# Last attention of a fused two-block transformer: compressed columns of a head pair in one pass, another home for the outputs' high parts, another filling order

## The chip, the cores and the metric

One core of one Trainium2 chip runs the whole program. The metric is the device time of one execution in microseconds (us). A change of less than half a per cent (about 5 us here) can't be told from no change.

## What is computed

Two transformer blocks over 256 tokens of width 1024, in fp32. The last layer's attention ("nsa") has 16 query heads over two groups of keys and values, and three branches for each head: compressed keys (15 columns, a small network over blocks of 32 tokens), selected keys (at 256 tokens every block is selected, so that this is plain causal attention) and a window (also all tokens). Each branch has a softmax of its own, and a gate:

```python
p_c = jax.nn.softmax(s_c, axis=-1) * c_valid
o_cmp = jnp.einsum('bhgsc,bchd->bshgd', p_c.astype(h.dtype), vc)
...
o = gates[..., 0:1] * o_cmp + gates[..., 1:2] * o_slc + gates[..., 2:3] * o_win
return o.reshape(B, S, ATTN_WIDTH) @ w_o
```

Then follow a residual sum, an RMS norm and a gated feed-forward layer.

## The kernel before

Activations lie transposed, features on partitions and 256 tokens along the row. Every weight is a slab of 128 x 1024 floats, streamed through twelve staging places. To keep fp32 precision in fast passes each operand is cut in two: ScalarE writes a rounded high part of a slab (`high_split`, L1087, eight places), VectorE the rest as a low part (`low_split`, L1601), and TensorE multiplies high by high, low by high and high by low. Each engine's program is written out by hand and runs in its order; semaphores tie them. The slab before use needs both parts.

The class `Splits` keeps the order of the slabs. `splits(n)` first calls `flush`, which writes on VectorE the low parts of all slabs whose high part has been issued since, and then issues n new high parts. `take` is called when a slab is about to be used; where its parts have not been issued yet, it issues them there and then:

```python
while j not in self.highs:
    self.next_high()
if j not in self.lows:
    self.flush()
```

The attention treats two heads (a pair) in a round, p = 0 to 9. For round p TensorE does `nsa_turn` of the pair before (transposes of the probabilities, L999 to L1008, the even head first, the odd one later), `nsa_products` (scores of pair p, L988, into banks 0 to 3), and `nsa_values` of pair p - 2 (L1023, L1027, into bank 6). VectorE does `nsa_scores` (bias, row maximum: L1945, six pieces of a head), `nsa_weights` (inverse sums times gates, scaling: L2228 to L2235) and `outs` (high and low part of the output row: L2244, L1949). ScalarE does `nsa_exp` (L1319) and copies the transposes out of PSUM (L1542 to L1548).

Between these pieces the `Filler` puts parts of other work, three times in a round, as many as `NSA_PARTS[p]` says: first the query tiles 2 to 7, each in three parts (24 matmuls: L521, L525, L529 to L538), all in bank 7, which is free again when VectorE has scaled the tile before (the third part on its queue, `nsa_query`, L1690); then the first products of the output projection (`part_of`, six matmuls each: L558 to L562), a slab of `nsa_o` and two of the eight output tiles at a time. On VectorE and ScalarE the same three places hold the slab splits (`NSA_SPLITS`). Before, each round of 0 to 5 holds one whole query tile, and rounds 6 to 9 hold 12 projection parts of the first four slabs. `project` then does the rest.

Of the kernel before, what the change touches and what calls it, by code (L numbers as in the profile page):

```python
# [11 lines left out]
STAG = 4  # L12
# [64 lines left out]
def _pack(inputs, sched):  # L77
# [86 lines left out]
    "lo", "low", "high_dve", "sums_dve", "x", "root_dve", "z", "top", "probabilities", "key_dve", "query_dve", "step",  # L164
# [154 lines left out]
def _program(nc, io, sched):  # L319
# [45 lines left out]
    bank = [nc.alloc_psum_tensor(f"bank{i}", [128, 512], F32) for i in range(8)]  # L365
# [69 lines left out]
    PC = work("PC", [128, 2, 2, 48], F32, 0)  # L435
# [47 lines left out]
    def attention_parts(p, more):  # L483

        return (1, 1, 1) if p < 6 else more[p - 6]
# [11 lines left out]
    def tensor(e):  # L497
# [79 lines left out]
        def project(name, rows, early, stage):  # L577
            for i in range(8 - STAG):
# [4 lines left out]
            ks = range(8 - STAG, 8)  # L583
            finish([take(name, i) for i in ks], rows, ks, stage)
# [297 lines left out]
        def values_turned(name, src, key):  # L882
# [3 lines left out]
            for m in range(2):  # L886
# [9 lines left out]
              lambda p, i: filler.parts(attention_parts(p, SWA_PARTS)[i]), lambda p: values_turned("swa values", VT, ("vt",)) if p == 0 else None)  # L896
# [19 lines left out]
        for m in range(2):  # L916
            p = e.transpose(bank[b][:, 64 * m:64 * m + 48], GR[:, 128 * m:128 * m + 128], idc[0:48, 0:48])
# [50 lines left out]
        for i in range(2):  # L968
# [6 lines left out]
                        + [(lambda x: part_of("nsa_o", outs, *x, early), (i, n)) for n in (0, 2, 4) for i in range(8 - STAG)])  # L975
        sums[:] = [7, 0, 1, 2]

        def nsa_products(p):

            k, x = KK[:, p // 4], QS[:, p % 4, :]  # L980
            q.wait_ge(*at("qs", "nsa", p))
            for key in (("kk zero",), ("kk half", 2, 1), ("kk half", 4, 1), ("kk", "c")):
                q.wait_ge(*at(*key))
            for i, (to, c, n, m, kc) in enumerate(((0, 0, 272, 1, 0), (0, 272, 144, 0, 256), (1, 0, 256, 1, 272), (1, 256, 128, 0, 0))):
                for o in range(2):
                    b = 2 * o + to
                    clear(b)
                    y = e.matmul(bank[b][:, c:c + n], x[HALF[o], 128 * m:128 * m + 128], k[HALF[o], kc:kc + n], start=True, stop=True)  # L988
                if i % 2:
                    y.then_inc(*up("scores", ("nsa scores", p, to)))  # L990
            for o in range(2):
                free[2 * o], free[2 * o + 1] = [("nsa read", 2 * p + o, 0)], [("nsa read", 2 * p + o, 1)]

        def nsa_turn(h):
            P, C = PN[:, h % 4], PC[:, h // 2 % 2]
            clear(4)
            q.wait_ge(*at("nsa probabilities", h, 0))
            for i, c in enumerate((512, 0, 128, 640)):
# [56 lines left out]
        project("nsa_o", outs, early, "mlp3")  # L1055
# [23 lines left out]
    def scalar(e):  # L1079
# [43 lines left out]
        def project(name, early, stage, g):  # L1123
            for i in range(8 - STAG):
# [3 lines left out]
            finish([slabs.take(name, i) for i in range(8 - STAG, 8)], stage, g)  # L1128
# [309 lines left out]
        def attention_fill(p, i, more, splits):  # L1438
            filler.parts(attention_parts(p, more)[i])
# [85 lines left out]
        for i in range(2):  # L1525
# [23 lines left out]

        for p in range(10):  # L1550
            if 1 <= p < 9:
# [17 lines left out]
        project("nsa_o", early, "mlp3", 6)  # L1569
# [23 lines left out]
    def vector(e):  # L1593
# [43 lines left out]
        def project(name, early, sums, stage, g, **more):  # L1637
            for i in range(8 - STAG):
# [3 lines left out]
            finish([slabs.take(name, i) for i in range(8 - STAG, 8)], sums, stage, g, **more)  # L1642
# [447 lines left out]
        def attention_fill(p, i, more, splits):  # L2090
            filler.parts(attention_parts(p, more)[i])
# [75 lines left out]
        e.tensor_scalar(GG[:, 0, 0:48:3], GG[:, 0, 0:48:3], late, None, ALU.mult).then_inc(*up("step", ("gates", 1)))  # L2167
# [31 lines left out]
        for i in range(2):  # L2199
# [6 lines left out]
                        + [(lambda i: part_of("nsa_o", i, early), i) for n in (0, 2, 4) for i in range(8 - STAG)])  # L2206

        def nsa_scores(h):
            a, b, slot = 2 * (h % 2), 2 * (h % 2) + 1, h % 4
            P, C, bt, o = PN[:, h % 4], PC[:, h // 2 % 2], BT[:, h, :], 32 * (h % 2)  # L2210
            if h >= 4:
                q.wait_ge(*at("nsa turned", h // 2 * 2 - 3, 1))
            q.wait_ge(*at("pc zero"))
            q.wait_ge(*at("bt2"))
            q.wait_ge(*at("nsa scores", h // 2, 0))
            top(P[:, 0:256], bank[a][:, 0:256], bt[:, 0:256], slot, 4, ("nsa top", h, 4))
            top(P[:, 640:768], bank[a][:, 288:416], bt[:, 128:256], slot, 2, ("nsa top", h, 2))
            top(C[:, 1, o:o + 15], bank[a][:, 256:271], bt[:, 31:256:16], slot, 3, ("nsa top", h, 3))
            top(C[:, 0, o:o + 7], bank[a][:, 272:279], bt[:, 159:256:16], slot, 0, ("nsa top", h, 0), ("nsa read", h, 0))
            q.wait_ge(*at("nsa scores", h // 2, 1))  # L2220
            top(P[:, 256:512], bank[b][:, 0:256], bt[:, 0:256], slot, 5, ("nsa top", h, 5))
            top(P[:, 512:640], bank[b][:, 256:384], bt[:, 128:256], slot, 1, ("nsa top", h, 1), ("nsa read", h, 1))

        def nsa_weights(h):
            slot, c, o = h % 4, 72 + 6 * (h % 4), 32 * (h % 2)
            P, C = PN[:, h % 4], PC[:, h // 2 % 2]
            q.wait_ge(*at("nsa exp", h, 1))
# [6 lines left out]
            for n, (i, x) in enumerate(((1, P[:, 512:640]), (4, P[:, 0:256]), (2, P[:, 640:768]), (5, P[:, 256:512]), (0, C[:, 0, o:o + 7]), (3, C[:, 1, o:o + 15]))):  # L2234
                x = e.tensor_scalar(x, x, row_stat(slot, 1, i), None, ALU.mult)  # L2235
                if n == 2:
                    x.then_inc(*up("probabilities", ("nsa probabilities", h, 0)))
                if n == 5:
                    x.then_inc(*up("probabilities", ("nsa probabilities", h, 1)))

        def outs(p):
            q.wait_ge(*at("values", "nsa", p))
            q.wait_ge(*at("slab", slab["swa_o", 7]))
            e.tensor_copy(OTH[:, p, :], bank[6][:, 0:256]).then_inc(*up("high_dve", ("o high", "nsa", p), ("high", "nsa out", p)))  # L2244
            out_low("nsa", p, 6)

        for p in range(10):
            if p < 8:
                nsa_scores(2 * p)
                nsa_scores(2 * p + 1)  # L2250
            attention_fill(p, 0, NSA_PARTS, NSA_SPLITS)
            if p < 8:
                nsa_weights(2 * p)
            attention_fill(p, 1, NSA_PARTS, NSA_SPLITS)
            if p >= 2:
                outs(p - 2)
            if p < 8:
# [22 lines left out]
    def gpsimd(e):  # L2280
# [115 lines left out]
        e.memset(BD[:, :, :], 0.0).then_inc(*up("pool_step", ("bd zero",)))  # L2396
        sum_squares("mlp3")
# [127 lines left out]
```

## Time and profile before

| what | value |
|---|---|
| median of 3 runs | 1002.12 us (1001.37 to 1005.74) |
| the profiled execution, its time | 1003.15 us |
| its span in the trace | 1001.3 us |
| TensorE matmul busy | 959.7 us, 96% |
| VectorE, ScalarE, GpSimd busy | 66%, 55%, 13% |
| mean granted clock of TensorE | 0.984 |

TensorE is busy nearly everywhere. In the page's forty slices it falls below nine tenths in the first three and in two later ones, and one of these is that of the last attention (about 702 to 802 us of the span). A busy matmul record says little of its pace: the granted clock has to be read beside it.

### The profile page before, as it was taken

Reading aid. Unit: us, or ns where it says so; the run is one execution under the profiler, and the core shown is the slowest. Engines: PE = TensorE matmul, PEld = TensorE weight load, DVE = VectorE, ACT = ScalarE, POOL = GpSimd, SP = SyncE. Lnnn points to the kernel's source line nnn. Section 1 sums busy time; section 2 is a strip of 40 time slices with the busy share of each in tenths; the row PEclk is TensorE's granted clock in tenths of the full one; section 3 lists DMA queues with packets and bytes.
Section 4 is the critical chain, followed back from the end, with each engine's and each line's share of the span. In section 5 each row is a group of like instructions: output and inputs, shape, how many; then the busy total and the mean of one; then the engine's idle time right before and its main releaser. Section 6 shows DMA issues by size and latency. Waiting matters only on the chain.

```text
span 1001.3 us, 19392 instructions
## 1 busy us (share of the span) xinstructions
PE 959.7 (96%) x7816; PEld 925.1 (92%) x7816; DVE 662.4 (66%) x1458; ACT 552.6 (55%) x1106; POOL 127.0 (13%) x131
## 2 busy tenths in 40 slices
PE   6958999999999999999999999999897999999997
PEld 6957999999999998879999999999786999999997
DVE  7769765666555556786865565668898477655552
ACT  5636663465445446785554444448798365444434
POOL 2010001230000003003221111210000121111111
PEclk8989999999999999999999999999899999999999
DMA  8994334497545544314964555557211255545521
GB/s 274 229 195 134 127 128 155 140 245 237 192 168 190 189 171 166 127 44 156 265 220 172 191 185 172 196 181 253 85 44 43 85 210 181 198 170 185 194 85 43
DMA packets 26537, 165.82 MB, mean 166 GB/s; under 512 B 3352, under 2 KB 4248, under 8 KB 8016
## 3 DMA queue, kind: packets, MB, share of 16 engines
q1 hardware_dynamic: 24048, 156.61, 45.5%
q0 software_dynamic: 2400, 7.97, 4.2%
q8 instruction: 62, 1.02, 0.4%
q14 instruction: 27, 0.22, 0.1%
HBM read 161.03 MB, written 3.01 MB: 164 GB/s over the span
## 4 chain that ended last, share of the span: by engine, by line
PE 81%; DVE 9%; ACT 5%; DMA 2%; issue 1%; SPq 0%; DVEq 0%; ACTq 0%
PE bank L521 12%; PE bank L525 12%; PE bank L529 12%; PE bank L558 9%; PE bank L562 9%; PE bank L560 9%; PE bank L533 4%; PE bank L532 4%; DVE lo L1601 2%; PE bank L538 2%; ACT PN L1319 2%; PE bank L536 2%; DMA K<-KR 1%; DMA stage<-in_stream 1%; PE bank L785 1%
## 5 line engine op out<-in xcount | busy, mean ns | idle before, releaser
L1601 DVE TENSOR_TENSOR lo<-stage,hi 128x1024 fp32r<-128x1024 f32 x291 | 346.8, 1223 | 9.8 <-ACT hi L1087 9.6
L1087 ACT ACTIVATE hi<-stage 128x1024 fp32r<-128x1024 f32 x291 | 299.6, 1045 | 59.6 <-PE bank L562 52.1
L558 PE MATMUL bank<-UH,hi 128*128 128x256 f32 x608 | 172.7, 284 | 0.4 <-ACT UH L1389 0.4
L562 PE MATMUL bank<-UL,hi 128*128 128x256 f32 x608 | 172.5, 284 | 0.0
L560 PE MATMUL bank<-UH,lo 128*128 128x256 f32 x608 | 172.4, 284 | 0.0
L521 PE MATMUL bank<-HTH,hi 128*128 128x256 f32 (+1 forms) x1038 | 158.2, 288 | 9.8 <-ACT HTH L1097 5.1
L525 PE MATMUL bank<-HTH,lo 128*128 128x256 f32 (+1 forms) x1038 | 155.3, 286 | 2.0 <-DVE lo L1601 2.0
L529 PE MATMUL bank<-HTL,hi 128*128 128x256 f32 (+1 forms) x1038 | 156.0, 287 | 0.0
L521 PEld LDWEIGHTS bank<-HTH,hi 128*128 128x128 f32 (+1 forms) x1038 | 137.6, 192 | 14.5 <-issue 6.2
L525 PEld LDWEIGHTS bank<-HTH,lo 128*128 128x128 f32 (+1 forms) x1038 | 137.3, 192 | 3.7 <-DVE lo L1601 2.6
L529 PEld LDWEIGHTS bank<-HTL,hi 128*128 128x128 f32 (+1 forms) x1038 | 137.7, 193 | 3.1 <-issue 3.0
L558 PEld LDWEIGHTS bank<-UH,hi 128*128 128x128 f32 x608 | 117.0, 192 | 0.6 <-issue 0.6
L562 PEld LDWEIGHTS bank<-UL,hi 128*128 128x128 f32 x608 | 116.9, 192 | 0.1
L560 PEld LDWEIGHTS bank<-UH,lo 128*128 128x128 f32 x608 | 117.0, 192 | 0.0
L2390 POOL TENSOR_TENSOR TH<-TH,RR 128x256 f32<-128x256 f32 x44 | 69.0, 1568 | 284.3 <-DVE TH L2112 284.3
L532 PE MATMUL bank<-HTH,hi 128*128 128x256 f32 (+2 forms) x346 | 98.2, 284 | 0.0
L533 PE MATMUL bank<-HTH,lo 128*128 128x256 f32 (+2 forms) x346 | 98.2, 284 | 0.0
L2291 POOL TENSOR_TENSOR SQ<-SQ 128x256 f32<-128x256 f32 x40 | 32.9, 831 | 427.1 <-ACT SQ L1103 425.9
L1389 ACT ACTIVATE UH<-U 128x256 fp32r<-128x256 f32 x76 | 31.7, 418 | 81.3 <-DVE U L2118 80.2
L2051 DVE TENSOR_TENSOR UL<-U,UH 128x256 fp32r<-128x256 f32 x76 | 32.3, 425 | 51.5 <-ACT UH L1389 51.5
L533 PEld LDWEIGHTS bank<-HTH,lo 128*128 128x128 f32 (+2 forms) x346 | 66.4, 192 | 0.0
L532 PEld LDWEIGHTS bank<-HTH,hi 128*128 128x128 f32 (+2 forms) x346 | 66.3, 192 | 0.0
(308 smaller groups left out, 1436.1 us busy)
## 6 DMA issues: line engine op xcount, KB each, us to landing
stage<-in_stream SPq DMA_DIRECT2D x144, 1024.0 KB, 4.9
BT<-scratch POOLq DMA_DIRECT2D x8, 256.0 KB, 15.7
BT<-scratch POOLq DMA_DIRECT2D x4, 512.0 KB, 19.6
stage<-in_stream SPq DMA_DIRECT2D x3, 512.0 KB, 10.2
scratch<-VR POOLq DMA_DIRECT2D x2, 768.0 KB, 21.5
XT<-in_xt SPq DMA_DIRECT2D x4, 256.0 KB, 6.5
B<-scratch POOLq DMA_DIRECT2D x4, 256.0 KB, 11.5
out<-ROWS SPq DMA_DIRECT2D x4, 256.0 KB, 2.4
```

The source lines that it names most:

```text
L521: e.matmul(out, wh[k], rows.high(k0 + k), start=k == 0, stop=False)
L525: e.matmul(out, wl[k], rows.high(k0 + k), start=False, stop=False)
L529: e.matmul(out, wh[k], rows.low(k0 + k), start=False, stop=False)
L532: e.matmul(out, wh[k], rows.high(k0 + k), start=False, stop=False)
L533: e.matmul(out, wl[k], rows.high(k0 + k), start=False, stop=False)
L558: e.matmul(out, hi[:, j % HI_SLOTS, c:c + 128], rows.high(k), start=start and n % 2 == 0, stop=False)
L560: e.matmul(out, lo[:, j // 2 % ST_PAIRS, j % 2, c:c + 128], rows.high(k), start=False, stop=False)
L562: last = e.matmul(out, hi[:, j % HI_SLOTS, c:c + 128], rows.low(k), start=False, stop=stop)
L1087: e.activation(hi[:, j % HI_SLOTS, 0:w], stage[:, j // 2 % ST_PAIRS, j % 2, 0:w], ACT.Copy).then_inc(*up("hi", ("hi", j, 0)))
L1601: e.tensor_tensor(lo[x], stage[x], f32(hi[:, j % HI_SLOTS, 0:sched[j][2]]), ALU.subtract).then_inc(*up("lo", ("lo", j, 0)))
L2291: e.tensor_tensor(sq[:, 0, :], sq[:, 0, :], sq[:, k, :], ALU.add).then_inc(*up("sums", ("squares so far", stage, c, k), *[("squares", stag ...
L2390: e.tensor_tensor(t, z, ROOT[stage], ALU.mult).then_inc(*up("silu", ("silu scaled", kind, f)))
```

## The change

- The compressed columns of both heads of a pair are read in one VectorE instruction from two neighbouring banks (`banks[:, 0:2, 256:288]`), with a bias table `BC` that GpSimd fills from `BT`; one maximum (`tensor_reduce`), one subtraction, one exponential on ScalarE without a sum, one sum on VectorE, and one scaling into `PC` for the four softmaxes. Before, these were four pieces of L1945, four of L1319 and four of L2235 in a pair. For it the heads of a pair use banks 0, 2 and 1, 3 rather than 0, 1 and 2, 3.
- The high part of the output row is copied by ScalarE (`nsa_out`) and no longer by VectorE; the low part stays on VectorE, now behind `nsa_weights` of the odd head.
- In round 1 TensorE does the products first and then the turn of head 0; in round 8 the values of pair 6 come first.
- `NSA_PARTS` and `NSA_SPLITS` change, and 20 projection parts of five slabs, all eight output tiles, are put in rather than 12 parts of four slabs.

```diff
-    SWA_PARTS, NSA_PARTS = ((1, 1, 1), (1, 1, 1), (1, 2, 2), (2, 2, 1)), ((1, 1, 0), (1, 1, 0), (0, 2, 2), (2, 1, 1))
+    SWA_PARTS = ((1, 1, 1),) * 8 + ((1, 2, 2), (2, 2, 1))
+    NSA_PARTS = ((2, 2, 1),) + ((1, 1, 1),) * 5 + ((1, 1, 0), (1, 0, 2), (4, 4, 0), (1, 1, 3))
...
-    NSA_SPLITS = ((0, 0, 1),) * 6 + ((0, 1, 1), (0, 1, 1), (1, 1, 1), (1, 1, 1))
+    NSA_SPLITS = ((0, 0, 0),) + ((0, 0, 1),) * 7 + ((1, 1, 0), (1, 1, 1))
...
-    def attention_parts(p, more):
-        return (1, 1, 1) if p < 6 else more[p - 6]
+    NSA_EARLY = 5
+    NSA_OUT_PARTS = [(i, n) for n in (0, 2, 4, 6) for i in range(NSA_EARLY)]
...
         for p in range(10):
-            if 1 <= p < 9:
+            if p == 8:
+                nsa_values(6)
+            if 2 <= p < 9:
                 nsa_turn(2 * p - 2)
             if p < 8:
                 nsa_products(p)
-            filler.parts(attention_parts(p, NSA_PARTS)[0])
+            if p == 1:
+                nsa_turn(0)
+            filler.parts(NSA_PARTS[p][0])
             if 1 <= p < 9:
                 nsa_turn(2 * p - 1)
-            filler.parts(attention_parts(p, NSA_PARTS)[1])
-            if p >= 2:
+            filler.parts(NSA_PARTS[p][1])
+            if p >= 2 and p != 8:
                 nsa_values(p - 2)
-            filler.parts(attention_parts(p, NSA_PARTS)[2])
+            filler.parts(NSA_PARTS[p][2])
...
+        def compressed_scores(p, step):
+            C = CC[:, p % 2].rearrange("p o (m c) -> p (o m) c", m=2)
+            if step == 0:
+                q.wait_ge(*at("bc"))
+                q.wait_ge(*at("nsa scores", p, 0))
+                e.tensor_tensor(CC[:, p % 2], banks[:, 0:2, 256:288], BC[:, 2 * p:2 * p + 2, :], ALU.add).then_inc(*up("step", ("compressed scores", p)))
+            if step == 1:
+                e.tensor_reduce(CM[:, p % 2], C, AX.X, ALU.max).then_inc(*up("step", ("compressed greatest", p)))
+            if step == 2:
+                e.tensor_tensor(C, C, CM[:, p % 2].unsqueeze(2).to_broadcast([128, 4, 16]), ALU.subtract).then_inc(*up("top", ("compressed less greatest", p)))
...
         for p in range(10):
             if p < 8:
-                nsa_scores(2 * p)
-                nsa_scores(2 * p + 1)
+                nsa_scores(p)
             attention_fill(p, 0, NSA_PARTS, NSA_SPLITS)
             if p < 8:
+                compressed_sums(p)
                 nsa_weights(2 * p)
             attention_fill(p, 1, NSA_PARTS, NSA_SPLITS)
-            if p >= 2:
-                outs(p - 2)
             if p < 8:
                 nsa_weights(2 * p + 1)
+            if p >= 2:
+                out_low("nsa", p - 2, 6)
             attention_fill(p, 2, NSA_PARTS, NSA_SPLITS)
```

On ScalarE `nsa_out(p - 2)` stands behind `nsa_exp(2 * p + 1)` and ahead of the third place for filling (in round 8 it stands first).

## Rows read from the trace of the kernel before

**Rows 1.** Waits of TensorE, 700 to 830 us: total, times, longest.

```profile
PE bank L999 <- DVE PN L2235: 5.0, 2, 2.6
PE bank L999 <- ACT PTN L1542: 2.6, 2, 2.4
PE bank L521 <- DVE QS L1690: 0.8, 1, 0.8
```

**Rows 2.** Timeline of TensorE, rounds 0 and 1: start, duration.

```profile
702.59 1.63 PE L988 MATMUL bank<-KK,QS 64*128 64x272 f32 x16
...
710.40 1.09 PE L999 MATMUL bank<-idc,PN 128*128 128x128 f32 x4 [2.58 <-DVE PN L2235]
...
711.85 3.04 PE L988 MATMUL bank<-KK,QS 64*128 64x272 f32 x16
```

**Rows 3.** Timeline of TensorE, one whole round in the middle.

```profile
729.46 1.63 PE L988 MATMUL bank<-KK,QS 64*128 64x272 f32 x16
731.01 0.97 PE L521 MATMUL bank<-HTH,hi 128*128 128x256 f32 x6
731.82 0.60 PE L999 MATMUL bank<-idc,PN 128*128 128x128 f32 x4
...
732.61 0.95 PE L525 MATMUL bank<-HTH,lo 128*128 128x256 f32 x6
733.50 0.87 PE L1023 MATMUL bank<-PTN,VS 128*64 128x256 f32 x8
...
735.57 0.98 PE L529 MATMUL bank<-HTL,hi 128*128 128x256 f32 x6
...
737.11 0.60 PE L999 MATMUL bank<-idc,PN 128*128 128x128 f32 x4
...
737.86 1.63 PE L988 MATMUL bank<-KK,QS 64*128 64x272 f32 x16
```

**Rows 4.** Timeline of TensorE, round 8.

```profile
774.42 1.11 PE L999 MATMUL bank<-idc,PN 128*128 128x128 f32 x4 [2.40 <-ACT PTN L1542]
```

**Rows 5.** Windows: length, TensorE busy (instructions), granted clock, DMA.

```profile
707.50:710.40 2.90, 0.32 (x6) 0.88 0.00 0
...
716.00:717.00 1.00, 1.00 (x9) 0.75 0.00 0
...
777.00:778.00 1.00, 1.00 (x7) 0.53 0.00 0
```

**Rows 6.** Timeline of VectorE, rounds 0, 1 and 5.

```profile
705.37 0.42 DVE L1945 CUSTOM_DVE_ANT_0 PN<-bank,BT 128x256 f32<-128x256 f32 x1
...
707.96 1.22 DVE L1601 TENSOR_TENSOR lo<-stage,hi 128x1024 fp32r<-128x1024 f32 x1
709.09 0.18 DVE L2228 RECIPROCAL small<-small 128x6 f32<-128x6 f32 x1
...
710.43 0.36 DVE L2235 TENSOR_SCALAR PC<-PC,small 128x7 f32<-128x7 f32 x2
...
722.13 0.42 DVE L1690 TENSOR_TENSOR QS<-bank,RR 128x256 f32<-128x256 f32 x1
...
747.39 0.42 DVE L1945 CUSTOM_DVE_ANT_0 PN<-bank,BT 128x256 f32<-128x256 f32 x1
```

**Rows 7.** The chain that ended last, merged pieces: start, duration.

```profile
719.02 0.57 ACT PC L1319 x4
719.60 0.89 ACT PN L1319 x4
...
772.95 0.95 ACT hi L1087
...
801.79 0.72 PE bank L521 x6
```

**Rows 8.** Timeline of TensorE at 22 us, a wait for a low part.

```profile
22.54 0.98 PE L525 MATMUL bank<-HTH,lo 128*128 128x256 f32 x6 [1.50 <-DVE lo L1601]
```

**Rows 9.** Windows after 22 us's wait: length, TensorE busy, granted clock.

```profile
20.00:30.00 10.00, 8.50 (x69) 1.00 1.01 301
```

More of the change, by code:

```diff
@@ L364, in _program @@
     posq = here_at("posq", [128, 2], I32, CS0 + 9184)
-    bank = [nc.alloc_psum_tensor(f"bank{i}", [128, 512], F32) for i in range(8)]
+    banks = nc.alloc_psum_tensor("banks", [128, 8, 512], F32)
+    bank = [banks[:, i, :] for i in range(8)]
     SQ = work("SQ", [128, 8, 256], F32, 0)
@@ L575, in finish, with project @@
                 after(b)
-        def project(name, rows, early, stage):
-            for i in range(8 - STAG):
+        def project(name, rows, early, stage, ahead=8 - STAG):
+            for i in range(ahead):
                 j = early[i] if i in early else take(name, i)
@@ L582, in project @@
                     accumulate_tile(j, rows, i, n, i == 0, False, [("slab", j)] if n == todo[-1] else ())
-            ks = range(8 - STAG, 8)
+            ks = range(ahead, 8)
             finish([take(name, i) for i in ks], rows, ks, stage)
@@ L1121, in finish, with project @@
                 slabs.give(j)
-        def project(name, early, stage, g):
-            for i in range(8 - STAG):
+        def project(name, early, stage, g, ahead=8 - STAG):
+            for i in range(ahead):
                 j = early[i] if i in early else slabs.take(name, i)
@@ L1127, in project @@
                 slabs.splits(2)
-            finish([slabs.take(name, i) for i in range(8 - STAG, 8)], stage, g)
+            finish([slabs.take(name, i) for i in range(ahead, 8)], stage, g)
         def part_of(name, i, early):
@@ L1438, in attention_fill @@
         def attention_fill(p, i, more, splits):
-            filler.parts(attention_parts(p, more)[i])
+            filler.parts(more[p][i])
             slabs.splits(splits[p][i])
@@ L1548, in nsa_turn, with nsa_out @@
             e.activation(PTN[:, h % 4, 512:768], bank[5][:, 0:256], ACT.Copy).then_inc(*up("pt", ("ptn", h, 1)))
+        def nsa_out(p):
+            q.wait_ge(*at("values", "nsa", p))
+            q.wait_ge(*at("slab", slab["swa_o", 7]))
+            e.activation(OTH[:, p, :], bank[6][:, 0:256], ACT.Copy).then_inc(*up("high", ("o high", "nsa", p), ("high", "nsa out", p)))
         for p in range(10):
+            if p == 8:
+                nsa_out(6)
             if 1 <= p < 9:
@@ L1635, in finish, with project @@
                 slabs.give(j)
-        def project(name, early, sums, stage, g, **more):
-            for i in range(8 - STAG):
+        def project(name, early, sums, stage, g, ahead=8 - STAG, **more):
+            for i in range(ahead):
                 j = early[i] if i in early else slabs.take(name, i)
@@ L1641, in project @@
                 slabs.splits(2)
-            finish([slabs.take(name, i) for i in range(8 - STAG, 8)], sums, stage, g, **more)
+            finish([slabs.take(name, i) for i in range(ahead, 8)], sums, stage, g, **more)
         def part_of(name, i, early):
@@ L2090, in attention_fill @@
         def attention_fill(p, i, more, splits):
-            filler.parts(attention_parts(p, more)[i])
+            filler.parts(more[p][i])
             if p > 0:
@@ new lines, in compressed_sums, with nsa_scores @@
+        def compressed_sums(p):
+            c = 72 + 6 * (2 * p % 4)
+            q.wait_ge(*at("compressed exp", p))
+            e.tensor_reduce(small[:, c:c + 12].rearrange("p (o m b) -> p o m b", o=2, m=2)[:, :, :, 0], CC[:, p % 2].rearrange("p o (m c) -> p o m c", m=2), AX.X, ALU.add).then_inc(*up("step", ("compressed sums", p)))
+        def nsa_scores(p):
+            q.wait_ge(*at("bt2"))
+            compressed_scores(p, 0)
+            for o in range(2):
+                h, a, b, slot = 2 * p + o, o, 2 + o, (2 * p + o) % 4
+                P, bt = PN[:, slot], BT[:, 2 * p + o, :]
+                if p >= 2:
+                    q.wait_ge(*at("nsa turned", 2 * p - 3, 1))
+                top(P[:, 0:256], bank[a][:, 0:256], bt[:, 0:256], slot, 1, ("nsa top", h, 1))
+                if o == 0:
+                    compressed_scores(p, 1)
+                top(P[:, 640:768], bank[a][:, 288:416], bt[:, 128:256], slot, 5, ("nsa top", h, 5), ("nsa read", h, 0))
+                if o == 0:
+                    compressed_scores(p, 2)
+                q.wait_ge(*at("nsa scores", p, 1))
+                top(P[:, 256:512], bank[b][:, 0:256], bt[:, 0:256], slot, 2, ("nsa top", h, 2))
+                top(P[:, 512:640], bank[b][:, 256:384], bt[:, 128:256], slot, 4, ("nsa top", h, 4), ("nsa read", h, 1))
@@ L2241, in outs @@
[L2241 to L2245, printed above, removed]
+            x.then_inc(*up("probabilities", ("nsa probabilities", h, 0)))
+            x = e.tensor_scalar(P[:, 256:512], P[:, 256:512], row_stat(slot, 1, 2), None, ALU.mult)
+            if h % 2:
+                p, c = h // 2, 72 + 6 * (h % 4 - 1)
+                q.wait_ge(*at("pc zero"))
+                if p >= 2:
+                    q.wait_ge(*at("nsa turned", 2 * p - 3, 1))
+                x = e.tensor_tensor(PC[:, p % 2].rearrange("p m (o c) -> p o m c", o=2)[:, :, :, 0:16], CC[:, p % 2].rearrange("p o (m c) -> p o m c", m=2),
+                                    small[:, c:c + 12].rearrange("p (o m b) -> p o m b", o=2, m=2)[:, :, :, 0:1].to_broadcast([128, 2, 2, 16]), ALU.mult)
```

76 lines of the change are left out of this document (38 added, 38 removed).

## The prediction, made before the changed kernel was run

> **What bounds the kernel now.** I read the page's slices first: TensorE is busy at 96%, so only its idle time and its slow time can be won. The waits of TensorE around the last attention come to 8.4 us in five places [rows 1]. Next its timeline. In a middle round the pieces stand back to back: products 1.55, first part of a query tile 0.81, turn of the odd head 0.79, second part 0.89, values 2.07, third part 1.54, turn of the even head 0.75, together 8.40 us without a gap [rows 3]. So in the middle TensorE is the bound, and a lighter VectorE or ScalarE wins nothing there. Then the two ends. Round 0 has only query tile 2 to hide the first softmax: it ends near 707.7 (0.4 us of compressed values included) and TensorE waits to 710.40 [rows 2], 2.7 us. Rounds 7 to 9 have waits of 2.5 and 2.4 [rows 1, 4] for the same reason. Last the granted clock: it fell to half within the first wait (0.88 mean over 2.9 us, so at 709.7) and came back at 716.5, 6.8 us later; after round 8 it came back at 777.9 [rows 5]. The products took 3.04 rather than 1.63 in it [rows 2, 3]. The slow stretches cost half of the work's time: (716.5 - 710.4)/2 = 3.05 and (777.9 - 774.4)/2 = 1.75, and some 0.3 in the turn ahead of it.
>
> Loss before: 2.7 + 3.05 + 0.8 (the wait for QS) + 4.9 + 1.75 + 0.3 + 0.2 (the short second wait of row 2 in [rows 1]) = 13.7 us. TensorE's work itself isn't changed: same matmuls, another order. The change is worth 13.7 minus what it loses after.
>
> **The lighter work on VectorE and ScalarE.** Per pair ScalarE loses four small exponentials, 2 x 0.57 [rows 7], and gains one of at most 0.29 and a copy near 0.42. VectorE loses four compressed pieces, about 0.4 together, four scalings (0.36 for two [rows 6], less what overlaps) and the cast of 0.45; it gains a read of both banks, a maximum, a subtraction, a sum and one scaling. I find no row for these; five bounds: 0.14 each (one scaling) to 0.25 each (a small one that waits for its forerunner; the reciprocal and its product take 0.42 for two). I take 0.2, so 1.0 against 1.4: 0.4 less. All of it lies beside TensorE in the middle. Not on any path: worth 0 by itself. GpSimd's two table copies stand behind the sum of squares that opens the layer, long before round 0; they cost nothing there, and a wait of VectorE ahead of 705.37 if I am wrong.
>
> **The start.** Parts (2, 2, 1) put five parts in round 0: query tile 2 and two thirds of tile 3. But tile 3 goes to bank 7 and needs QS(2), and that is now in the second place for filling on VectorE, behind `nsa_weights(0)`. On VectorE: scores start at 705.37 and took 2.59 to the split at 707.96 [rows 6]; new 2.75 (2.2 for eight large pieces, three small ones), to 708.1; split 1.13; sums 0.2; weights 1.34 (709.09 to 710.43), to 710.8; QS 0.42: 711.25. TensorE has ended tile 2 at 707.15 and waits 4.1 us, where it waited 2.7. The clock falls as before and returns at 716.5: (716.5 - 711.3)/2 = 2.6. The wait of 0.8 goes. Together 6.7, against 6.55 before: nothing won. (Bounds of the small ones: 6.5 to 7.)
>
> **The new phase of the query tiles.** From round 1 each round holds the third part of one tile and two of the next. The first of these needs QS, which stands on VectorE behind all scores of the round. TensorE is there 1.54 + 0.79 = 2.33 after the products' end, 3.88 after their start. VectorE can begin scores 1.13 after that start (747.39, products at 746.26 by the period [rows 3, 6]), takes 2.75, QS 0.42: 4.3. So a wait of 0.45 in rounds 3, 4 and 5 (0.2 to 0.8 by the bounds), 1.35. In round 2 VectorE is late, as ScalarE's turn of head 0, now behind the products, holds up exp(2) to 720.6 and with it weights(3) to 725.0: scores to 727.75, QS to 728.2, TensorE ready at 726.55: 1.65. Sum 3.0. Before, QS stood ahead of two pieces (2.3 us of TensorE) and its wait was nought after round 1.
>
> **The split slabs, which I think decide.** The front page's `Splits` can be worked. At the attention's start the high parts up to query tile 5 are issued. Before: one split in each of rounds 0 to 5 gives q6, q7, o0 to o3 (slabs of the projection), and o0 is wanted in round 6, long after. After: none in round 0, one in 1 to 7: q6, q7, o0, o1, o2 (end of round 5). The parts then take o0 and o1 in round 5 (ready), o2 and o3 in round 6, o4 in round 7. o2's low part is flushed in round 6's first place, behind all scores. o3 isn't issued at all: `take` issues its high part on ScalarE behind turn(11), its low part on VectorE after it. o4 has its high part from the end of round 6, its low part again behind the scores of round 7. TensorE wants each of them at once. With the products of round 6 ending at 760.75 (756.21, three rounds of 8.40 behind 731.01 [rows 3], plus 1.5 of two parts done ahead, plus the 3 lost):
> - (o2): scores from 760.3 to 763.1, low part 1.22 to 764.3. TensorE waits from 761.1: 3.2.
> - (o3): turn(11) ends 767.1 at half clock, its copies 768.0, high part 0.95 [rows 7] to 769.0, low part 770.2. TensorE ready at 767.2: 3.0.
> - (o4): the products end 778.4 (values, turn and products, most at half clock), scores 780.8, low part 782.0; TensorE ready 778.5: 3.5.
> - Values(6) ahead of round 8 need bank 6, read by the low part of output 5, behind weights(15), behind exp(15): VectorE gets there near 789.5; TensorE at 789.8: 0 here, but 2.7 if the three waits above weren't there.
> Waits 9.7. At half clock from about 763.5: the work between the waits, 2.8 us long, 1.4 lost; after the second wait a spell of 6.8 with work all through, 3.4; after the third 5.8 of it with work, 2.9. Sum 7.7. A wait of 1.5 us for a low part left the clock at full [rows 8, 9], the waits of 2.5 and 2.7 didn't, so 3 us should cost it.
>
> The Trainium skill ("TensorE: Matmul & The Clock Gate", Part 1) says the same of the chip: idle time throttles the array to 1.2 GHz and only sustained work brings back 2.4 GHz. It speaks against a change that makes one wait into three. By that rule the sum holds; were the clock left at full, it would be 7.7 less. The traces bear the rule out in both ends of this attention.
>
> **Sum.** After: 6.7 + 3.0 + 9.7 + 7.7 = 27.1; minus 13.7: 13.4 slower. A second way: from 789.8 on the rest stands without a wait (values 2.07, turns 1.54, 8 parts 5.8, 2 parts 1.45, values 2.07, 3 parts 2.2, 24 products of three slabs 8.65: 23.7), so the feed-forward starts at 813.5 rather than 801.79 [rows 7]: 11.7. Between them 12.5. Behind it nothing changes: the projection's slabs come free about 1 us later against its end. On the profiled execution's 1003.15 that is 1015.6; this one lies 1.0 above the median, so a median of 1014.6. I take 1014.
>
> **The rivals.**
> 1. The clock stays at full in the late waits, as they are broken by work (for: the 1.5 us wait; against: 2.5 and 2.7 fell). Then 27.1 - 7.7 = 19.4, but without slow work values(6) wait 0.9: +6.6, 1008.7. 18%.
> 2. The end fills as it is meant to: the low parts of o2 to o4 are there in time, because the splits run ahead of what I worked out (one in hand by round 6 is enough). Price: 17.4 of late loss becomes the wait of values(6), 2.7, and its clock 3.4; the sum 15.8 against 13.7, +2: no change, 1004, 7%. If that wait is short too, 9.7: 4 faster, 998, and 5 to 6 faster, 997, with the cheap end of VectorE's small ones (phase waits 0.2); 7% for both, the side beyond 0.5% 5%. It decides from the point where the three waits and their clock together fall below 4. Against: the order of the queues.
> 3. Worse: the clock stays half from 763 to the end of round 8, and the phase wait is 0.8 each: +17 to +20, 1020. 12%.
> The forecast itself: 56%, 1009 to 1018.
>
> **Numbers.** 1014. The range leaves out the faster case, half of "no change" and half of rival 3: 1003 to 1019. A change under 0.5%, 5 us, can't be told from none. Faster by more: 0.05. Within (997.1 to 1007.1): the rest of rival 2, 0.09, and the lower edge of rival 1, 0.05: 0.14. Slower: 0.81.
>
> **What would show it.** Right: TensorE's first wait near 4 us and released by QS; short waits for QS in rounds 2 to 5; two or three waits of L560 (low part) of about 3 us around 761 to 782, released by L1601; in them VectorE in L1945; clock at 0.5 in more of the slices there. Wrong: no wait on L560, or the two ends filled without gaps; QS ahead of the turn; a round in the middle unlike 8.40 for VectorE's sake.

## The result, and the profile after

The changed kernel takes 1012.87 us (median of 4 runs, 1012.16 to 1017.84), the one before 1002.41 (4 runs). The medians lie 10.5 us apart, where 12 were forecast; the ratio over all runs is 1.0124, with a 95% interval of 1.0095 to 1.0154. The profiled execution took 1012.64 us with a span of 1010.8, 9.5 longer than before.

All of it lies in and just behind the last attention. From the first products of the attention (702.59 before, 702.33 after) to the second gate tile of the feed-forward (805.19 and 814.67) it is 102.60 us before and 112.34 after, 9.74 more. I call this stretch the stage below, since it leaves out what differs between executions in the first hundred microseconds. (In the forty slices of the kernel before, both of the later low ones, from 700.9 and from 751.0 us, lie in it, and not one.)

The waits of TensorE in the changed kernel, 700 to 840 us, the three largest groups (who for whom: total, times, longest); they answer to [rows 1]:

```profile
PE banks L565 <- DVE lo L1622: 6.8, 3, 3.0
PE banks L526 <- DVE QS L1711: 5.0, 2, 3.9
PE banks L563 <- ACT hi L1096: 1.7, 1, 1.7
```

The two long waits for probabilities and that of 2.4 us for ScalarE's copy are gone, as was meant. In their place stand three for the low part of a slab, one for a high part, and one of 3.9 us for QS. On TensorE's timeline they are these (start, duration, and in brackets the idle time before); the first answers to the second row of [rows 2], the last to [rows 4]:

```profile
710.92 1.35 PE L526 MATMUL banks<-HTH,hi 128*128 128x256 f32 x6 [3.90 <-DVE QS L1711]
...
726.95 0.98 PE L526 MATMUL banks<-HTH,hi 128*128 128x256 f32 x6 [1.06 <-DVE QS L1711]
...
762.41 0.52 PE L565 MATMUL banks<-OTH,lo 128*128 128x256 f32 x1 [2.98 <-DVE lo L1622]
...
767.17 0.38 PE L563 MATMUL banks<-OTH,hi 128*128 128x256 f32 x1 [1.68 <-ACT hi L1096]
768.43 0.39 PE L565 MATMUL banks<-OTH,lo 128*128 128x256 f32 x1 [0.88 <-DVE lo L1622]
...
778.65 0.39 PE L565 MATMUL banks<-OTH,lo 128*128 128x256 f32 x1 [2.98 <-DVE lo L1622]
```

L565 is the second matmul of a projection part: its slab's high part was there, its low part not. What VectorE did meanwhile shows why. The timeline of VectorE in round 6, from the last piece of the scores on:

```profile
760.92 0.29 DVE L1966 CUSTOM_DVE_ANT_0 PN<-banks,BT 128x128 f32<-128x128 f32 x1
761.13 1.22 DVE L1622 TENSOR_TENSOR lo<-stage,hi 128x1024 fp32r<-128x1024 f32 x1
...
767.15 1.23 DVE L1622 TENSOR_TENSOR lo<-stage,hi 128x1024 fp32r<-128x1024 f32 x1 [3.19 <-ACT hi L1096]
```

The split of o2 stands straight behind the scores, and TensorE goes on 0.06 us after its end at 762.35. The split of o3 has waited 3.2 us for ScalarE, and ScalarE's high part (from 766.07 on) stood behind the copies of turn(11), which TensorE could only do once it had o2. So each late slab makes the next one late.

The granted clock of those waits (windows: length, TensorE busy, clock, DMA), against [rows 5]:

```profile
711.00:712.00 1.00, 1.00 (x6) 0.66 0.00 0
...
714.00:715.00 1.00, 1.00 (x9) 0.64 0.00 0
762.00:763.00 1.00, 0.59 (x3) 0.76 0.00 0
765.00:766.00 1.00, 0.49 (x3) 0.54 0.00 0
769.00:770.00 1.00, 1.00 (x7) 0.67 0.00 0
772.00:773.00 1.00, 1.00 (x3) 0.62 0.00 0
779.00:780.00 1.00, 1.00 (x10) 0.79 0.05 16
782.00:783.00 1.00, 1.00 (x10) 0.51 0.00 0
```

Between the two windows of each pair the clock was at its lower level, 1.2 GHz. With the means taken apart, the four spells are 711.3 to 714.7, 762.5 to 765.9, 769.3 to 772.8 and 779.6 to 783.0: 3.4 us each. Each begins 0.1 to 1.0 us behind the end of a wait: of 3.90, of 2.98, of the pair 1.68 and 0.88, and of 2.98 us. Both spells of the kernel before took 6.8. Its second began at 771.1, behind the wait that ended at 770.80, and went on through the wait of 2.40 us [rows 4] to 777.9, so that one spell served two waits:

```profile
771.00:772.00 1.00, 1.00 (x6) 0.56 0.00 0
```

The end of the stage changed too, which was not foreseen. VectorE there, in the changed kernel:

```profile
799.17 0.42 DVE L1970 TENSOR_TENSOR OTL<-banks,OTH 128x256 fp32r<-128x256 f32 x1 [3.90 <-ACT OTH L1565]
800.12 4.63 DVE L1622 TENSOR_TENSOR lo<-stage,hi 128x1024 fp32r<-128x1024 f32 x4 [0.52 <-ACT hi L1096]
804.66 0.75 DVE L1639 TENSOR_TENSOR XT<-banks,XT 128x256 f32<-128x256 f32 x2
```

and in the kernel before:

```profile
789.30 3.50 DVE L1601 TENSOR_TENSOR lo<-stage,hi 128x1024 fp32r<-128x1024 f32 x3 [1.89 <-ACT hi L1087]
793.19 0.76 DVE L1618 TENSOR_TENSOR XT<-bank,XT 128x256 f32<-128x256 f32 x2 [0.39 <-PE bank L562]
```

Before, VectorE waited 0.39 us for the first sum of the projection. After, it went from four splits rather than three straight into that sum, so the sum had been waiting for it; and with three slabs at the end rather than four the further sums come faster (before, VectorE waited 0.94 and 0.99 us for the third and fourth pair of them, after for none). TensorE pays at the first gate tile, which needs the rows made of these sums:

```profile
809.53 0.64 PE L526 MATMUL banks<-HTH,hi 128*128 128x256 f32 x4
810.41 0.79 PE L526 MATMUL banks<-HTH,hi 128*128 128x256 f32 x2 [0.24 <-ACT HTH L1106]
...
814.67 1.06 PE L526 MATMUL banks<-HTH,hi 128*128 128x256 f32 x6
```

and in the kernel before:

```profile
801.63 0.88 PE L521 MATMUL bank<-HTH,hi 128*128 128x256 f32 x6
...
805.19 1.06 PE L521 MATMUL bank<-HTH,hi 128*128 128x256 f32 x6
```

From the first to the second gate tile it is 5.14 us, against 3.56 before: 1.6 lost.

### The profile page after: what moved, and what is told of

Same layout as the page of the kernel before. It is cut to its first block, busy times and chain, and to the rows that moved or that the text cites. A ratio compares the mean times of both kernels' runs of the same rounds, so it can differ in the third digit from the quotient of the medians.

```text
span 1010.8 us, 19272 instructions
## 1 busy us (share of the span) xinstructions
PE 964.5 (95%) x7816; PEld 927.4 (92%) x7816; DVE 658.2 (65%) x1394; ACT 549.1 (54%) x1058; POOL 129.1 (13%) x134
## 4 chain that ended last, share of the span: by engine, by line
PE 84%; DVE 9%; ACT 3%; DMA 2%; issue 1%; SPq 0%; DVEq 0%
PE banks L530 12%; PE banks L526 12%; PE banks L534 12%; PE banks L563 9%; PE banks L565 9%; PE banks L567 9%; PE banks L538 4%; PE banks L537 4%; DVE lo L1622 3%; PE banks L543 2%; PE banks L541 2%; DMA K<-KR 1%; PE banks L1028 1%; PE banks L790 1%; PE banks L776 1%
## 5 line engine op out<-in xcount | busy, mean ns | idle before, releaser
L563 PE MATMUL banks<-UH,hi 128*128 128x256 f32 x608 | 172.3, 283 | 0.4 <-ACT UH L1398 0.4
L526 PE MATMUL banks<-HTH,hi 128*128 128x256 f32 (+1 forms) x1038 | 158.8, 288 | 14.5 <-ACT HTH L1106 5.7
L567 PE MATMUL banks<-UL,hi 128*128 128x256 f32 x608 | 172.2, 283 | 0.0
L565 PE MATMUL banks<-UH,lo 128*128 128x256 f32 x608 | 172.0, 283 | 0.0
L530 PE MATMUL banks<-HTH,lo 128*128 128x256 f32 (+1 forms) x1038 | 155.8, 286 | 1.2 <-DVE lo L1622 1.2
L526 PEld LDWEIGHTS banks<-HTH,hi 128*128 128x128 f32 (+1 forms) x1038 | 138.0, 192 | 19.8 <-DVE QS L1711 6.0
L534 PE MATMUL banks<-HTL,hi 128*128 128x256 f32 (+1 forms) x1038 | 155.8, 286 | 0.0
L530 PEld LDWEIGHTS banks<-HTH,lo 128*128 128x128 f32 (+1 forms) x1038 | 138.1, 193 | 3.8 <-issue 2.2
L534 PEld LDWEIGHTS banks<-HTL,hi 128*128 128x128 f32 (+1 forms) x1038 | 137.7, 192 | 1.7 <-issue 1.2
L563 PEld LDWEIGHTS banks<-UH,hi 128*128 128x128 f32 x608 | 116.7, 192 | 0.6 <-issue 0.6
L565 PEld LDWEIGHTS banks<-UH,lo 128*128 128x128 f32 x608 | 116.7, 192 | 0.0
## 6 DMA issues: line engine op xcount, KB each, us to landing
stage<-in_stream SPq DMA_DIRECT2D x3, 512.0 KB, 10.3
```

Source lines behind the costliest of these rows:

```text
L526: e.matmul(out, wh[k], rows.high(k0 + k), start=k == 0, stop=False)
L530: e.matmul(out, wl[k], rows.high(k0 + k), start=False, stop=False)
L534: e.matmul(out, wh[k], rows.low(k0 + k), start=False, stop=False)
L563: e.matmul(out, hi[:, j % HI_SLOTS, c:c + 128], rows.high(k), start=start and n % 2 == 0, stop=False)
L565: e.matmul(out, lo[:, j // 2 % ST_PAIRS, j % 2, c:c + 128], rows.high(k), start=False, stop=False)
L567: last = e.matmul(out, hi[:, j % HI_SLOTS, c:c + 128], rows.low(k), start=False, stop=stop)
```

## The experiments

Each stage length is read from that kernel's own trace, from its first products to its second gate tile: one execution, so that a low spell of the clock that lasted longer in it is in the figure. Ratios are to the kernel before on the same chip.

| kernel | median us | ratio (95%) | stage us |
|---|---|---|---|
| before | 1001.1 to 1002.4 | 1 | 102.60 |
| changed | 1012.87 | 1.0124 (1.0095 to 1.0154) | 112.34 |
| x1_splits | 1007.29 | 1.0052 (1.0036 to 1.0068) | 105.13 |
| x2_whole_tiles | 1003.21 | 1.0013 (1.0004 to 1.0023) | 102.29 |
| x3_light | 1000.77 | 0.9988 (0.9979 to 0.9998) | 100.87 |
| x4_order | 1014.15 | 1.0113 (1.0096 to 1.0130) | 114.48 |
| x5_values_back | 995.57 | 0.9946 (0.9926 to 0.9966) | 95.11 |
| x6_two_tiles | 996.17 | 0.9949 (0.9933 to 0.9966) | 96.35 |
| x7_four_slabs | 993.18 | 0.9921 (0.9904 to 0.9937) | 93.63 |
| x8_heavy | 995.06 | 0.9939 (0.9922 to 0.9955) | 95.31 |
| x9_spread | 994.78 | 0.9944 (0.9930 to 0.9957) | 94.43 |
| x10_late_splits | 999.33 | 0.9985 (0.9970 to 1.0000) | 98.40 |

The two halves of the change apart came first: the lighter work alone, in the old order (x3), and the order alone, with the old work (x4).

```diff
# x3_light, from the changed kernel: order, parts, splits, slabs of before
-    NSA_PARTS = ((2, 2, 1),) + ((1, 1, 1),) * 5 + ((1, 1, 0), (1, 0, 2), (4, 4, 0), (1, 1, 3))
-    NSA_SPLITS = ((0, 0, 0),) + ((0, 0, 1),) * 7 + ((1, 1, 0), (1, 1, 1))
-    NSA_EARLY = 5
-    NSA_OUT_PARTS = [(i, n) for n in (0, 2, 4, 6) for i in range(NSA_EARLY)]
+    NSA_PARTS = ((1, 1, 1),) * 6 + ((1, 1, 0), (1, 1, 0), (0, 2, 2), (2, 1, 1))
+    NSA_SPLITS = ((0, 0, 1),) * 6 + ((0, 1, 1), (0, 1, 1), (1, 1, 1), (1, 1, 1))
+    NSA_EARLY = 4
+    NSA_OUT_PARTS = [(i, n) for n in (0, 2, 4) for i in range(NSA_EARLY)]
...
-            if p == 8:
-                nsa_values(6)
-            if 2 <= p < 9:
+            if 1 <= p < 9:
                 nsa_turn(2 * p - 2)
```

```diff
# x4_order, from the kernel before: the same lines the other way, compressed columns and casts untouched
+    NSA_PARTS = ((2, 2, 1),) + ((1, 1, 1),) * 5 + ((1, 1, 0), (1, 0, 2), (4, 4, 0), (1, 1, 3))
-    NSA_SPLITS = ((0, 0, 1),) * 6 + ((0, 1, 1), (0, 1, 1), (1, 1, 1), (1, 1, 1))
+    NSA_SPLITS = ((0, 0, 0),) + ((0, 0, 1),) * 7 + ((1, 1, 0), (1, 1, 1))
+    NSA_EARLY = 5
```

> The kernel before with only the merged compressed columns and the output's high part on ScalarE; order, parts, splits and four early slabs of before. Theory A (TensorE sets the middle, the lighter engines only shorten the waits at the ends): 0 to 2 us faster, 1000 to 1002.5. Theory B (the lighter engines carry the stage): 5 us faster or more.

> The kernel before with only the new order, parts, splits and five early slabs; compressed columns and output casts as before. Theory A (the whole loss is in the order): as slow as the changed kernel or up to 4 us slower, since VectorE reaches the low parts later: 1012 to 1017. Theory B (the merged pieces cost it): within 3 us of the kernel before.

The lighter work alone is 0.12% faster (0.02 to 0.21%), as theory A had it, and less than the half per cent that can be told from nothing; its stage is 1.7 us shorter. Of that only 0.6 us are waits, 8.5 in the kernel before and 7.9 in x3: the wait of 0.8 for QS is gone, and the first wait, in round 0, is even longer, 2.85 against 2.58. Most of the rest is the first low spell of the clock, 3.4 us in x3 (710.0 to 713.4) and 6.8 in the kernel before, worth 1.35 us; no run shows that the lighter work shortened it. The order alone gives all of the loss, 114.5 us of stage, 2.1 over the changed kernel. Two of its waits for a low part are longer (3.05 and 3.63 us against 2.98 twice) and one is shorter (0.68 against 0.88), the wait for QS in round 2 is 1.68 rather than 1.06, and its first low spell took 6.8 us rather than 3.4. So the order costs, and the merge costs nothing.

**The splits.** x1 takes the changed kernel and puts back the old plan for the slabs, and nothing else:

```diff
-    NSA_SPLITS = ((0, 0, 0),) + ((0, 0, 1),) * 7 + ((1, 1, 0), (1, 1, 1))
+    NSA_SPLITS = ((0, 0, 1),) * 6 + ((0, 1, 1), (0, 1, 1), (1, 1, 1), (1, 1, 1))
```

> The changed kernel with the slab splits of before (one from round 0 on, two in rounds 6 and 7); all else as changed. Theory A (the low and high parts of slabs o2, o3, o4 come too late): the three waits of TensorE for them (2.98, 1.68 + 0.88, 2.98 us) and their slow clock (about 4.9) go, 13.4 us; in their place the values of pair 6 wait for bank 6, 2 to 3 us, and some clock, so 1002 to 1006. Theory B (VectorE is simply behind there and would let TensorE wait for something else just as long): 1010 to 1013.

The stage falls by 7.2 us, and the median of 1007.3 lies 1.3 over what theory A gave, far from theory B. The stage didn't fall by 13, for two reasons. Two short waits for low parts are left: that of o3 stands behind the scores of round 6, that of o4 in the last place of it. And the values of pair 6, which the change puts ahead of round 8, now wait, which they didn't while TensorE was late itself. The timeline of TensorE in x1:

```profile
762.32 0.39 PE L565 MATMUL banks<-OTH,lo 128*128 128x256 f32 x1 [1.40 <-DVE lo L1622]
...
768.34 0.39 PE L565 MATMUL banks<-OTH,lo 128*128 128x256 f32 x1 [0.42 <-DVE lo L1622]
...
777.03 1.55 PE L1028 MATMUL banks<-PTN,VS 128*64 128x256 f32 x8 [3.26 <-issue]
```

"issue" says that the trace names nobody. VectorE's timeline does: its low part of output 5, the last reader of bank 6, runs from 776.51 to 776.93, and TensorE starts 0.1 us behind it. The clock fell there too (776.4 to 779.8), which costs 1.4 us.

**Whole tiles in a round.** x2 adds to x1 the old phase of the query tiles, with the 20 parts in the rounds behind:

```diff
-    NSA_PARTS = ((2, 2, 1),) + ((1, 1, 1),) * 5 + ((1, 1, 0), (1, 0, 2), (4, 4, 0), (1, 1, 3))
+    NSA_PARTS = ((1, 1, 1),) * 6 + ((1, 1, 1), (1, 1, 2), (4, 4, 0), (1, 1, 3))
```

> As x1_splits, and the query tiles again whole in rounds 0 to 5, so that the scaling QS stands at the end of the round on VectorE; rounds 6 to 9 hold all 20 projection parts as (1,1,1), (1,1,2), (4,4,0), (1,1,3). Theory A: the wait of 3.9 us in round 0 and the QS waits (1.06 and three of 0.26) go, and the products of round 1 fill the wait for the first softmax, so 5 to 8 us under x1_splits: 995 to 999. Theory B (the first softmax sets the start whatever is filled in): within 2 us of x1_splits.

2.8 us less of stage, not 5 to 8, and 1003.2 rather than 995 to 999. The wait of 3.9 us became two of 1.2, though the clock still fell for 3.4 us (710.8 to 714.2), and the later waits for QS and for low parts went. But the wait for bank 6 grew to 4.12 us, as TensorE got there earlier, and the clock stayed low from 768.8, within that wait, to 779.1. TensorE's timeline and two windows of x2:

```profile
709.29 0.66 PE L1004 MATMUL banks<-idc,PN 128*128 128x128 f32 x4 [1.20 <-DVE PN L2278]
...
711.36 1.65 PE L526 MATMUL banks<-HTH,hi 128*128 128x256 f32 x6 [1.20 <-DVE QS L1711]
...
770.73 1.55 PE L1028 MATMUL banks<-PTN,VS 128*64 128x256 f32 x8 [4.12 <-issue]
```

```profile
768.00:769.00 1.00, 0.00 (x0) 0.91 0.00 0
...
779.00:780.00 1.00, 1.00 (x10) 0.97 0.00 0
```

**The values of pair 6.** x5 is x2 with that one step, and ScalarE's copy that belongs to it, back in its place:

```diff
         for p in range(10):
-            if p == 8:
-                nsa_values(6)
...
-            if p >= 2 and p != 8:
+            if p >= 2:
                 nsa_values(p - 2)
```

> x2_whole_tiles with the values of pair 6 (and their copy) back in their old place, behind the eight parts of round 8. Theory A (ahead of round 8 they wait for bank 6, which the low part of output 5 frees only behind exp(15) and weights(15)): the wait of 4.12 us there goes and the slow clock behind it (some 9 us of work at half pace, 4.6) too; 7 to 9 us under x2: 994 to 996. Theory B (rounds 7 and 8 wait for the last softmax in any order): the wait moves to the turns L1004, less than 3 us won.

7.2 us less of stage, within what A gave: the wait of 4.12 and half of the 8.3 us at the low clock behind it, 8.3 together, less a wait of 0.62 (L1004) that came in its place, about 7.7. In this order, one step drawn ahead cost that much.

**The start, and the number of early slabs.** x6 does two whole query tiles in round 0, the second in bank 5, which nobody uses then; x7 is x6 with four early slabs:

```diff
# x6_two_tiles, from x5
-    NSA_PARTS = ((1, 1, 1),) * 6 + ((1, 1, 1), (1, 1, 2), (4, 4, 0), (1, 1, 3))
+    NSA_PARTS = ((3, 2, 1),) + ((1, 1, 1),) * 4 + ((1, 1, 0), (0, 1, 1), (1, 0, 2), (4, 4, 0), (1, 1, 3))
-        filler = Filler([(lambda i: tile_in_parts("nsa_q", i, next_bank, rows), i) for i in range(2, 8)]
+        filler = Filler([(lambda i: tile_in_parts("nsa_q", i, lambda: 5 if i == 3 else 7, rows), i) for i in range(2, 8)]
# x7_four_slabs, from x6
-    NSA_PARTS = ((3, 2, 1),) + ((1, 1, 1),) * 4 + ((1, 1, 0), (0, 1, 1), (1, 0, 2), (4, 4, 0), (1, 1, 3))
-    NSA_EARLY = 5
+    NSA_PARTS = ((3, 2, 1),) + ((1, 1, 1),) * 4 + ((1, 1, 0), (0, 1, 1), (0, 0, 3), (3, 3, 0), (1, 1, 1))
+    NSA_EARLY = 4
```

(A tile's bank is also marked as busy at its third part already, since a turn may now take it before the next part.)

> x5_values_back with query tiles 2 and 3 both whole in round 0, tile 3 in bank 5, so that it need not wait for QS(2); two projection parts in rounds 5 and 6. Theory A (the start lacks work that waits for nobody): the waits of 1.2 and 1.2 us and the slow stretch of 2.3 us in round 0 and 1 go, so 3 to 5 us under x5: 990 to 993. Theory B (the work is only moved: rounds 5 and 6 now wait for VectorE as long): within 1.5 us of x5.

> x6_two_tiles with four early slabs of the projection (16 parts) rather than five (20). Theory A (five early slabs leave three for the end, whose four sums then come faster than VectorE, with five splits ahead of them, can add and split them; seen as 1.6 us more before the second gate tile): 1 to 2.5 us under x6. Theory B (the end costs the same): within 0.7 us of x6, or slower where a wait comes back in round 8.

x6 missed: 1.2 us more of stage than x5, and a median within theory B. The start is as hoped, with no wait before 716.5 us and the clock full. But with less work in round 6 TensorE reached the first place of round 7, and o4 in it, before VectorE had come to o4's low part in the last place of round 6. The same fault was back:

```profile
762.28 0.38 PE L565 MATMUL banks<-OTH,lo 128*128 128x256 f32 x1 [1.87 <-DVE lo L1620]
```

with a slow spell (763.6 to 767.0) behind it. x7, which has no such part, has four waits of 0.6 to 1.0 us and one of 0.2 left and no slow window in the whole stage. It is the fastest: 0.9921 of the kernel before, and 19.7 us under the changed one by the medians. Of the 2.7 us of stage between x6 and x7 1.6 lie between the two gate tiles (5.15 against 3.56). In the rest, the waits are about as long in both (3.6 and 3.7 us), and x6 has the low spell. All kernels with four early slabs have 3.56 there, all with five 5.1 but x4, 4.6.

**The merge in the good order**, and **late splits in the good order** are the two tests the other way round. x8 is x7's order (tile 3 in bank 5 and the values of pair 6 in their old place included, which the lines below leave out) with the old compressed columns and casts; x10 is x7 with the changed kernel's `NSA_SPLITS`:

```diff
# x8_heavy, from x4_order
-    NSA_PARTS = ((2, 2, 1),) + ((1, 1, 1),) * 5 + ((1, 1, 0), (1, 0, 2), (4, 4, 0), (1, 1, 3))
-    NSA_SPLITS = ((0, 0, 0),) + ((0, 0, 1),) * 7 + ((1, 1, 0), (1, 1, 1))
-    NSA_EARLY = 5
+    NSA_PARTS = ((3, 2, 1),) + ((1, 1, 1),) * 4 + ((1, 1, 0), (0, 1, 1), (0, 0, 3), (3, 3, 0), (1, 1, 1))
+    NSA_SPLITS = ((0, 0, 1),) * 6 + ((0, 1, 1), (0, 1, 1), (1, 1, 1), (1, 1, 1))
+    NSA_EARLY = 4
# x10_late_splits, from x7_four_slabs
-    NSA_SPLITS = ((0, 0, 1),) * 6 + ((0, 1, 1), (0, 1, 1), (1, 1, 1), (1, 1, 1))
+    NSA_SPLITS = ((0, 0, 0),) + ((0, 0, 1),) * 7 + ((1, 1, 0), (1, 1, 1))
```

> The order, parts and splits of x7_four_slabs with the compressed columns and output casts of the kernel before. Theory A (TensorE sets the stage once it has work at both ends, VectorE has 0.4 us a round to spare or not): 0 to 3 us over x7. Theory B (the merge is what lets the order work): over 4 us above x7.

> x7_four_slabs with the split plan of the changed kernel (none in round 0, one a round up to 7): o2's low part is then flushed in the first place of round 6 and wanted in the second, o3's high and low part are issued where TensorE wants it. Theory A (late splits cost what they cost in the changed kernel): two or three waits for L1096 and the low split together 3 to 6 us, and 1 to 3.5 us of slow clock: 4 to 9 us over x7. Theory B (the order elsewhere was the cause): within 2 us of x7.

The merge is worth 1.7 us of stage here (95.31 against 93.63), 1.9 by the medians, though the intervals of the two ratios overlap. Neither trace has a low spell, and here it is all waits: 5.2 us in x8, 3.7 in x7. That x3 gave the same 1.7, most of it the clock, is chance. Late splits cost 4.8 us of stage, and the ratio goes from 0.9921 to 0.9985, some 6 us. The waits are those expected, and one of 1.40 for the low part of o1 ahead of them:

```profile
758.25 0.39 PE L565 MATMUL banks<-OTH,lo 128*128 128x256 f32 x1 [2.15 <-DVE lo L1620]
...
762.59 0.38 PE L563 MATMUL banks<-OTH,hi 128*128 128x256 f32 x1 [1.42 <-ACT hi L1096]
763.85 0.38 PE L565 MATMUL banks<-OTH,lo 128*128 128x256 f32 x1 [0.87 <-DVE lo L1620]
```

**What x7 has left.** x9 spreads the parts again, (0, 0, 4) and (3, 2, 0) in rounds 7 and 8, and puts the first turn ahead of the products:

```diff
-    NSA_PARTS = ((3, 2, 1),) + ((1, 1, 1),) * 4 + ((1, 1, 0), (0, 1, 1), (0, 0, 3), (3, 3, 0), (1, 1, 1))
+    NSA_PARTS = ((3, 2, 1),) + ((1, 1, 1),) * 4 + ((1, 1, 0), (0, 1, 1), (0, 0, 4), (3, 2, 0), (1, 1, 1))
...
-            if 2 <= p < 9:
+            if 1 <= p < 9:
                 nsa_turn(2 * p - 2)
             if p < 8:
                 nsa_products(p)
-            if p == 1:
-                nsa_turn(0)
```

> x7_four_slabs with four parts of the projection in round 7 and (3, 2, 0) in round 8, and the turn of head 0 ahead of the products again. Theory A (the waits that are left in x7, 1.00 and 0.57 and 1.04 us at the even turns for VectorE's scaling and 0.81 for ScalarE's copy, are each a want of work ahead of the turn): 0.5 to 2 us under x7, 991 to 993. Theory B (VectorE and ScalarE bound rounds 5 to 8 by now): the waits only move, within 0.5 us of x7.

0.8 us more of stage. The wait of 1.04 at the turn of head 14 fell to 0.33 and the 0.23 behind it went, but turn(0) now waits 0.29 and then 1.35 for bank 5 (TensorE's L1012 for QS): the theory was right for round 8 and wrong for the start. The two edits weren't run apart. In rounds 5 and 6, with two parts a round, TensorE still waits for VectorE and ScalarE (0.15, 0.58 and 0.82 us in x9); whether work taken from elsewhere could fill that wasn't tried.

## Why the prediction was right, point by point

The time, 1012.87, lies within the range, and its way was right. The steps, forecast against measured:

| step | forecast | measured |
|---|---|---|
| VectorE's scores with the merged pieces | 2.75 | 2.61 (705.10 to 707.71) |
| wait in round 0 for QS | 4.1 | 3.90 |
| its slow clock | 2.6 | 1.7 |
| round 2 late, and the phase of the tiles | 1.65 + 3 x 0.45 | 1.06 + 0.27 + 3 x 0.26 |
| low part of o2 | 3.2 | 2.98 |
| high and low part of o3 | 3.0 | 1.68 + 0.88 |
| low part of o4 | 3.5 | 2.98 |
| values of pair 6 | 0 behind the others | 0 |
| slow clock of rounds 6 and 7 | 7.7 | 4.9 |
| behind the projection | 0 | 1.6 |
| sum, less 13.7 of before | 13.4 | 9.0 (the stage grew by 9.7) |

In the row of round 2, 0.27 is a wait of turn(2) for VectorE's scaling, which wasn't forecast. Of the stage's growth 0.7 us are in none of the rows. The phase wait is read from the products' starts in the chain of work of the changed kernel, one round apart: 8.66 and 8.67 us, where it was 8.40 [rows 3].

```profile
731.57 1.56 PE banks L993 x16
...
740.23 1.56 PE banks L993 x16
...
748.90 1.56 PE banks L993 x16
```

**The mechanism** was right in each place that the prediction named, and the experiments show it: the splits by x1 and x10, the phase and round 0 by x2, the values of pair 6 (a wait that appears only once the others are gone, 2.7 forecast, 3.3 and 4.1 measured) by x1, x2 and x5.

**The sizes** were off in one way. The slow clock was mis-sized: I took a spell of 6.8 us for each wait, from the two of the kernel before [rows 5], and here each took 3.4. It cost 1.7, 1.5, 1.7 and 1.7 us, 6.6 where 10.3 were forecast. The waits were 2.3 us shorter in all than forecast. The rule of the Trainium skill that was weighed ("TensorE: Matmul & The Clock Gate", Part 1), that idle time brings the lower clock, agrees with this trace: the clock fell within 1.0 us of the end of all three waits of about 3 us or more, and of the pair of 1.68 and 0.88. How long it stays low isn't the same each time: 3.4 us four times here, 6.8 twice before, 10.2 in x2 from within the wait of 4.12. Nor does the wait's length decide alone. x2's two waits of 1.2 us with 0.9 of work between them brought it down, four of 0.6 to 1.0 in x7, with over 2 us of work between any two, didn't. The wait of 1.87 in x6 was followed by a low spell, that of 2.15 in x10 wasn't: the mean clock of x10 from 748 to 764 us is 1.00.

**A term that was missing**: "Behind it nothing changes" was wrong by 1.6 us, and "0" stood in the sum for it. I had checked when the slabs come free, and not what VectorE does between them: four splits rather than three ahead of the first sum. That the loss goes with the fifth early slab is shown by the kernels above; which of the two, the extra split or the quicker sums, takes how much of the 1.6 wasn't tried. Nor is it all the slab's: x4, with five slabs and the high part of the output still on VectorE, loses 1.0. In the changed kernel ScalarE begins with the last high parts (799.03) only behind its copy of the last output (798.75), and VectorE waits 0.52 us for the first of them, as its line above shows; in x4 ScalarE has two of them done by then, and VectorE doesn't wait. That this makes the other 0.6 fits, and wasn't tried alone.

**Luck.** The errors stand against each other: the waits and the clock that were foreseen came to 6.0 us less than forecast, and the missed 1.6 hid part of that. By its own sum the prediction gave 13.4 where 9.0 can be counted; that 1014 lies so near to 1012.87 is in part chance.

**VectorE's small pieces.** Taken at 0.2 from bounds of 0.14 and 0.25, they cost the lower one when other work stands between them and what they wait for. Timeline of VectorE, round 0:

```profile
705.10 0.22 DVE L2235 TENSOR_TENSOR CC<-banks,BC 128x64 f32<-128x64 f32 x1
705.23 0.41 DVE L1966 CUSTOM_DVE_ANT_0 PN<-banks,BT 128x256 f32<-128x256 f32 x1
...
705.57 0.21 DVE L2238 TENSOR_REDUCE CM<-CC 128x4 f32<-128x64 f32 x1
705.70 0.28 DVE L1966 CUSTOM_DVE_ANT_0 PN<-banks,BT 128x128 f32<-128x128 f32 x1
...
705.91 0.22 DVE L2241 TENSOR_TENSOR CC<-CC,CM 128x64 f32<-128x64 f32 x1
706.05 0.42 DVE L1966 CUSTOM_DVE_ANT_0 PN<-banks,BT 128x256 f32<-128x256 f32 x1
```

Each takes 0.13 or 0.14 us from its start to the next one's. And the lighter work wasn't worth quite 0, as I had it: 0.6 us of waits in the old order (x3) and 1.6 in the good one (x7 against x8). "Not on any path" overlooked that the waits at the ends hang on these engines.

## What to carry to other kernels

When work is drawn forward to fill a gap, draw its inputs forward too: follow each operand back through the queue of the engine that makes it, and count by hand in which place it is issued. Here one split fewer in round 0, and one rather than two in rounds 6 and 7, made three slabs late, which cost 7.2 us of stage (x1) or 4.8 (x10). It wasn't the only fault: the values of pair 6 drawn ahead cost 7.2 once the splits were right (x5), and rounds without whole query tiles 2.8 (x2). Without these, and with four early slabs, the same kind of change is 0.8% faster than the kernel before (x7), where it was 1.2% slower.

A wait that is removed uncovers the next: the values of pair 6 cost nothing in the changed kernel, 3.3 us in x1 and 4.1 in x2. Judge each part of such a change in the order that the others leave, and take the moved step out by itself.

## What the runs showed of the hardware

The length of the clock's low spell was 3.4 us (all four of the changed kernel), 6.8 (both of the kernel before, one each in x3 and x4) or 10.2 (x2, 768.8 to 779.1; x4, 765.1 to 775.4). It differed at waits of one length: at that of 3.90 us in round 0 it was 3.4 in the changed kernel and 6.8 in x4 (710.5 to 717.3). So a price taken from one trace was off by a factor of two here. A read of 64 columns out of two PSUM banks in one VectorE instruction takes 0.22 us, as much as one of 64 out of SBUF (the subtraction, 0.22).
